# A two-layer encoder step in float32: expert token rows fetched by an indirect DMA, and expert weights split 2048 columns at a time into three pairs of buffers

## Chip, cores and metric

One NeuronCore of a Trainium2 chip runs the whole program. The metric is the device time of one execution in microseconds; lower is better. TensorE (PE) multiplies matrices, VectorE (DVE) and ScalarE (ACT) work element by element, GpSimd (POOL) and SyncE (SP) here mostly start DMAs.

## What is computed

The program is one inference step of a two-layer trunk on 256 prompt tokens and 32 sample tokens (288 columns, `TOK`), width 1024, all in float32. Each layer is a mixer with three gated branches and a feed-forward part; the second layer's feed-forward is a mixture of 8 experts, of which each token uses 2. The change concerns that last part:

```python
def moe(h, w_router, b_router, w1, w3, w2):
    logits = jnp.einsum('...d,de->...e', h, w_router) + b_router
    top_v, top_i = lax.top_k(logits, TOP_K)                 # TOP_K = 2 of N_EXPERTS = 8
    top_w = jax.nn.softmax(top_v, axis=-1)
    combine = jnp.einsum('...k,...ke->...e', top_w, jax.nn.one_hot(top_i, N_EXPERTS))
    y = None
    for e in range(N_EXPERTS):
        term = combine[..., e:e + 1] * swiglu(h, w1[e], w3[e], w2[e])   # w1, w3: 1024 x 3584, w2: 3584 x 1024
        y = term if y is None else y + term
    return y
```

## The kernel before, in words

**Float32 as two halves.** Every weight is used as a sum of a rounded part (`w_hi`) and a remainder (`w_lo`), both in the type float32r, and so is every activation. A product takes three matmuls: high by high, high by low, low by high. ACT makes `w_hi` (line 766 in the expert stage), DVE makes `w_lo` by a subtraction (line 1169), and PE multiplies.

**Jobs, turns, chunks.** The expert stage works through jobs. A job is one expert with up to 128 of its tokens (slots); with these inputs there are 8 jobs. A job has 7 turns (`TURNS`), a turn has two units of 256 hidden features, and a turn uses 6 weight matrices of 1 MB, each cut into two chunks of 1024 columns. PE takes the chunks of a turn in this order: `unit_rows(0)` chunks 0 to 3, `unit_down` chunks 4 and 5 (they belong to the unit before), `turn_hidden(0)`, `unit_rows(1)` chunks 6 to 9, `unit_down` chunks 10 and 11, `turn_hidden(1)`. A chunk is six matmuls of 512 columns.

**Buffers.** SP loads matrices into a ring of six 1 MB slots (`expert_ring`); a slot is loaded anew when DVE has split its second chunk. There are four `w_hi` and four `w_lo` buffers of 1024 columns (`CHUNKS`). ACT may round chunk c when PE has used chunk c-4. Within a turn ACT and DVE go through chunks 4 to 15, of which 12 to 15 are the first four of the next turn.

**Between the chunks**, in an order written out by hand in `turn_work`, ACT applies SiLU to the gate (`silu_unit`, line 944) when PE has finished `unit_rows`, DVE multiplies (`silu_times_g`, line 1518), PE transposes the result (`turn_hidden`, line 1929), ACT and DVE split it (`hidden_high`, `hidden_low`), and `unit_down` uses it. All engines run their own program in order and wait on semaphores.

**Job boundaries.** Results of job j are scaled and split in turn 0 of job j+1 (`sums_high`, `sums_low`) and scattered back to tokens by PE two row blocks at a time (`scatter`, line 1977), through the two `SPARE` PSUM banks. DVE adds each block to `x` (`add_rows`, line 1551) and so frees the bank. `scatter(2, 3)` at the head of turn 1 waits for `add_rows(0, 1)`, and `turn_spread` (line 1986) at its end waits for `add_rows(6, 7)`.

**Gathering tokens.** `spread` is a 0/1 matrix of tokens by slots. In turn 6 of a job, `gather(1)` (line 1887) multiplies it with the token rows `h_tok_hi` and `h_tok_lo`, 12 matmuls of 512 columns; ACT copies the result to `he_rows`, and `turn_rows` (line 1898) transposes it, since the experts want features on partitions. `gather(0)` does it for the first job right after the router. `low_rows` (line 1448) makes `h_tok_lo` on DVE within the router's chain.

Of the kernel before, what the change touches and what calls it, by code (L numbers as in the profile page):

```python
# [14 lines left out]
P = 128  # L15
D = 1024
DT = D // P
# [30 lines left out]
CHUNKS = 4  # L48
JOB_CHUNKS = 6 * UNITS
# [3 lines left out]
PEELED = 2  # L53
# [145 lines left out]
def number_groups():  # L199
# [8 lines left out]
    g.add([("logits",)] + [("htok", n, h) for h in range(2) for n in range(3)] + [("columns",), ("counts",)])  # L208
# [9 lines left out]
class Turns:  # L218
# [26 lines left out]
    def buffer(self, c):  # L245

        return (c - self.skipped(c)) % CHUNKS

# [8 lines left out]
def encoder(nc, x_t, vecs, w_in, cache_k_t, cache_v, ws_t, bs, g_v, bias_t, bias_s, w_branch, w_out,  # L257
            w1, w3, w2, router, router_b, e_w, y_t, k_t, v_t, z_state, vn_rows):
# [3 lines left out]
    with ctx:  # L262
# [3 lines left out]
        def sem(name):  # L266
# [17 lines left out]
        rows6 = sb("rows6", [P, 6, HALF])  # L284
# [28 lines left out]
        w_hi = [sb(f"w_hi{i}", [P, CHUNK_W], f32r) for i in range(CHUNKS)]  # L313
        w_lo = [sb(f"w_lo{i}", [P, CHUNK_W], f32r) for i in range(CHUNKS)]
# [15 lines left out]
        primed = sb("primed", [P, 1])  # L330
        rwg = sb("rwg", [P, DT, EXPERTS])
# [19 lines left out]
        h_tok_hi, h_tok_lo = sb("h_tok_hi", [P, 3, D], f32r), sb("h_tok_lo", [P, 3, D], f32r)  # L351
# [5 lines left out]
        rows_flat = rows6[:, :, :].rearrange("p a b -> p (a b)")  # L357
        sq = rows_flat[:, 0:DT * TOK].rearrange("p (a b) -> p a b", a=DT)
# [82 lines left out]
        htok_high, htok_low = sem("htok_high"), sem("htok_low")  # L441
        spread_ready, gathered, he_rows_ready, he_turned = (
            sem(n) for n in ("spread_ready", "gathered", "he_rows_ready", "he_turned"))
# [32 lines left out]
        def reader(name):  # L476
# [10 lines left out]
            if kind == "htok":  # L487
                return htok_low, 3 * at[1] + at[0] + 1
# [119 lines left out]
        def _(pool):  # L608
# [9 lines left out]
                           allow_small_or_imprecise_dtypes=True).then_inc(made, 1)  # L618
            pool.wait_ge(pool_step, 3)
# [45 lines left out]
            pool.wait_ge(state_stored, 64)  # L665


        @block.scalar
        def _(act):
# [99 lines left out]
            def drained_chunks(work, *chunks):  # L769
                at = turns.turn  # L770
                turns.turn, turns.drained = TURNS, True
                work(*chunks)
                turns.turn, turns.drained = at, False
# [1349 lines left out]
```

## Time and profile before

| | us |
|---|---|
| median of 3 runs | 1870.42 |
| lowest and highest of them | 1867.22 and 1872.52 |
| the profiled execution | 1872.94 |
| its span, first to last instruction | 1870.9 |
| what lies around the span | 2.0 |
| from the start of the first `gather` to the end of the span | 1047.1 |

The profile is of one execution. It lists each instruction with its start and its duration and, for an engine that stood idle, what ended the idle time. The expert stage takes more than half of the span and starts, with the first `gather`, at 823.81 us. PE is busy for 98% of the span and DVE for 77%; in the expert stage both are close to full. A matmul's busy time overlaps with that of the next one, so PE's stalls are better read from the starts of the weight loads (PEld) than from the busy share. "x6" behind an instruction means that six of its kind are merged in that row. The instructions of the spare and ring slots are the same operation on different buffers.

### The profile page before, as it was taken

What the parts mean: (1) busy time and instruction counts of PE and PEld (TensorE: products, weight loads), DVE (VectorE), ACT (ScalarE), POOL (GpSimd) and SP (SyncE); (2) the same over time, 40 slices, a digit from 0 to 9 for tenths busy, and PEclk for the clock granted to TensorE, in tenths of its full rate; (3) what the DMA queues carried; (4) which work ended last, traced back from release to release, by engine and by line L of the source; (5) the groups of instructions that cost most, each with busy time, mean ns of one, the idle gap of its engine ahead of it and who ended that gap; (6) DMA issues with size and microseconds to landing.
All of it is one profiled execution on the core that took longest, in us unless ns stands there. A gap on an engine that the chain in (4) does not pass through costs nothing.

```text
span 1870.9 us, 30255 instructions
## 1 busy us (share of the span) xinstructions
PE 1828.3 (98%) x10461; PEld 1601.4 (86%) x10461; DVE 1441.1 (77%) x1930; ACT 1165.0 (62%) x1551; POOL 24.7 (1%) x46
## 2 busy tenths in 40 slices
PE   8999999999999999989999999999999999999997
PEld 8999999999998999957878788788788787887886
DVE  7563557766665645549989989899899898998997
ACT  5444445333455433438877777778778777777785
POOL 3000000000000000000000000000000000000000
PEclk9999999999999999979999999999999999999999
DMA  8444533444544334148989989889899899898993
GB/s 333 150 136 143 196 136 140 168 172 153 180 148 150 113 136 158 68 180 339 374 320 345 373 317 353 330 336 365 335 340 376 319 345 373 313 355 322 345 375 134
DMA packets 68816, 479.05 MB, mean 256 GB/s; under 512 B 7888, under 2 KB 9936, under 8 KB 11520
## 3 DMA queue, kind: packets, MB, share of 16 engines
q1 hardware_dynamic: 66256, 469.00, 67.0%
q0 software_dynamic: 2336, 8.90, 1.4%
q8 instruction: 55, 0.90, 0.2%
q14 instruction: 25, 0.20, 0.0%
q10 hardware_dynamic: 144, 0.04, 0.0%
HBM read 474.23 MB, written 3.69 MB: 255 GB/s over the span
## 4 chain that ended last, share of the span: by engine, by line
PE 88%; DVE 7%; issue 3%; ACT 1%; DVEq 0%; DMA 0%; SPq 0%; ACTq 0%
PE psum L1939 14%; PE psum L1782 12%; PE psum L1784 12%; PE psum L1783 12%; PE psum L1919 10%; PE psum L1921 10%; PE psum L1920 10%; DVE w_lo L1169 2%; PE psum L1887 2%; PE psum L1929 1%; PE psum L1642 1%; DVE w_lo L1091 1%; PE psum L1977 0%; ACT w_hi L766 0%; PE psum L1898 0%
## 5 line engine op out<-in xcount | busy, mean ns | idle before, releaser
L1169 DVE TENSOR_TENSOR w_lo<-ring,w_hi 128x1024 fp32r<-128x1024 f32 x448 | 541.2, 1224 | 47.1 <-ACT w_hi L766 18.5
L766 ACT ACTIVATE w_hi<-ring 128x1024 fp32r<-128x1024 f32 x448 | 475.4, 1065 | 113.2 <-PE psum L1921 86.2
L1091 DVE TENSOR_TENSOR w_lo<-ring,w_hi 128x1024 fp32r<-128x1024 f32 x218 | 266.4, 1224 | 250.2 <-ACT w_hi L681 250.2
L681 ACT ACTIVATE w_hi<-ring 128x1024 fp32r<-128x1024 f32 x218 | 230.6, 1060 | 338.1 <-PE psum L1784 336.1
L1919 PE MATMUL psum<-w_hi,h_hi 128*128 128x512 f32 x896 | 359.8, 402 | 0.7 <-ACT h_hi L960 0.7
L1921 PE MATMUL psum<-w_hi,h_lo 128*128 128x512 f32 x896 | 351.0, 392 | 0.0
L1920 PE MATMUL psum<-w_lo,h_hi 128*128 128x512 f32 x896 | 350.1, 391 | 0.0
L1782 PE MATMUL psum<-h_hi,w_hi 128*128 128x288 f32 x1120 | 336.8, 301 | 11.6 <-DVE h_lo L1202 7.0
L1783 PE MATMUL psum<-h_lo,w_hi 128*128 128x288 f32 x1120 | 332.2, 297 | 0.0
L1784 PE MATMUL psum<-h_hi,w_lo 128*128 128x288 f32 x1120 | 331.2, 296 | 0.0
L1169 DVE TENSOR_TENSOR w_lo<-spare,w_hi 128x1024 fp32r<-128x1024 f32 x224 | 271.6, 1223 | 45.5 <-ACT w_hi L766 43.1
L766 ACT ACTIVATE w_hi<-spare 128x1024 fp32r<-128x1024 f32 x224 | 237.2, 1063 | 61.7 <-PE psum L1921 38.0
L1782 PEld LDWEIGHTS psum<-h_hi,w_hi 128*128 128x128 f32 x1120 | 211.7, 189 | 17.5 <-issue 9.7
L1784 PEld LDWEIGHTS psum<-h_hi,w_lo 128*128 128x128 f32 x1120 | 212.6, 190 | 0.0
L1783 PEld LDWEIGHTS psum<-h_lo,w_hi 128*128 128x128 f32 x1120 | 212.2, 190 | 0.0
L1921 PEld LDWEIGHTS psum<-w_hi,h_lo 128*128 128x128 f32 x896 | 168.7, 188 | 36.9
L1919 PEld LDWEIGHTS psum<-w_hi,h_hi 128*128 128x128 f32 x896 | 168.9, 189 | 33.2 <-ACT h_hi L960 1.0
L1920 PEld LDWEIGHTS psum<-w_lo,h_hi 128*128 128x128 f32 x896 | 169.4, 189 | 32.3
L1939 PE MATMUL psum<-w_hi,hid_hi 128*128 128x512 f32 x444 | 137.7, 391 | 0.0
L1939 PE MATMUL psum<-w_lo,hid_hi 128*128 128x512 f32 x444 | 137.2, 390 | 0.0
L1939 PE MATMUL psum<-w_hi,hid_lo 128*128 128x512 f32 x444 | 137.0, 390 | 0.0
L1939 PEld LDWEIGHTS psum<-w_hi,hid_lo 128*128 128x128 f32 x444 | 83.3, 188 | 17.9
(274 smaller groups left out, 2220.0 us busy)
## 6 DMA issues: line engine op xcount, KB each, us to landing
ring<-in_e_w SPq DMA_DIRECT2D x224, 1024.0 KB, 4.8
spare<-in_e_w SPq DMA_DIRECT2D x112, 1024.0 KB, 4.9
ring<-in_w_in SPq DMA_DIRECT2D x56, 1024.0 KB, 4.8
ring<-in_w SPq DMA_DIRECT2D x33, 1024.0 KB, 4.8
ring<-in_w_branch SPq DMA_DIRECT2D x12, 1024.0 KB, 4.8
ring<-in_w_out SPq DMA_DIRECT2D x8, 1024.0 KB, 4.8
bias<-in_bias_t POOLq DMA_DIRECT2D x2, 1024.0 KB, 9.9
x<-in_x_t SPq DMA_DIRECT2D x4, 288.0 KB, 3.9
```

Of the source, the lines that this page charges most:

```text
L681: nc.scalar.activation(dst, src, ACT.Copy).then_inc(rounded, 1)
L766: nc.scalar.activation(w_hi[turns.buffer(c)][:, :], expert_ring[s][:, c % 2 * CHUNK_W:(c % 2 + 1) * CHUNK_W], ACT.Copy).then_inc(rounded, 1)
L1091: nc.vector.tensor_tensor(low, src, high.bitcast(f32), ALU.subtract).then_inc(split, 1)
L1169: nc.vector.tensor_tensor(w_lo[buf][:, :], expert_ring[s][:, c % 2 * CHUNK_W:(c % 2 + 1) * CHUNK_W], w_hi[buf][:, :].bitcast(f32), ALU.sub ...
L1782: nc.tensor.matmul(bank(name), high, high_src[k], start=(k == 0), stop=False)
L1783: nc.tensor.matmul(bank(name), high, low_src[k], start=False, stop=False)
L1784: ins = nc.tensor.matmul(bank(name), low, high_src[k], start=False, stop=(k == tiles - 1))
L1887: ins = nc.tensor.matmul(psum[:, SPARE[hf], :], spread[0:rows, n, :], source[0:rows, n, cols], start=(n == 0 and source is h_tok_hi), stop ...
L1919: nc.tensor.matmul(out, he_hi[:, k, :], w_high, start=(k == 0), stop=False)
L1920: nc.tensor.matmul(out, he_hi[:, k, :], w_low, start=False, stop=False)
L1921: ins = nc.tensor.matmul(out, he_lo[:, k, :], w_high, start=False, stop=(k == DT - 1))
L1939: ins = nc.tensor.matmul(psum[:, SUMS[hf], :], h_part[:, b, :], w_part[:, hf * 512:(hf + 1) * 512], start=(first and b == 0 and w_part is ...
```

## The change

Token rows are written once to DRAM (`token_rows`, 288 rows and a row of zeros), by three DMAs on ACT's queue. For each job PE multiplies `spread` with a column of token numbers (`find_rows`, three matmuls with one column), DVE turns the result into integers (`row_numbers`), and POOL starts an indirect DMA that reads the rows named there from DRAM into `he_rows`. This replaces the 12 matmuls of `gather`, ACT's copies in `gathered_rows` and DVE's `low_rows`. For a later job `find_rows(1)` stands in turn 2 in place of turn 6, and the third turn is peeled off the loop for it. On DVE `row_numbers(1)` stands in turn 2 between the chunk pairs 4 and 6. In all 12 indirect DMAs are issued, as many as there can be jobs.

The expert weights are rounded and subtracted 2048 columns at a time (`round_pair`, `low_pair`), which is a whole matrix or two chunks, into three pairs of buffers: six chunks, where there were four. The third `w_lo` pair lies over `rows6`, and the third `w_hi` pair takes the room of `h_tok_lo`. The dense layers still split 1024 columns at a time in the first four buffers.

```diff
 CHUNK_W = 1024
 CHUNKS = 4
+EXPERT_CHUNKS = 6
...
-PEELED = 2
+PEELED = 3
...
     def buffer(self, c):
-        return (c - self.skipped(c)) % CHUNKS
+        return (c - self.skipped(c)) % EXPERT_CHUNKS
...
+            pool.wait_ge(rows_written, 48)
+            for job in range(MAX_JOBS):
+                pool.wait_ge(slot_row_ready, job + 1)
+                if job:
+                    pool.wait_ge(gathered, 16 * job)
+                nc.gpsimd.indirect_dma_start(he_rows, None, token_rows, bass.IndirectOffsetOnAxis(ap=slot_row[:, 0:1], axis=0),
+                                             bounds_check=TOK).then_inc(gathered, 16)
+            pool.wait_ge(gathered, 16 * MAX_JOBS)
...
+            def round_pair(c, drained=False):
+
+                at, s = turns.turn, c // 2 % EXPERT_RING
+                turns.turn, turns.drained = (TURNS, True) if drained else (at + c // TURN_CHUNKS, False)
+                c %= TURN_CHUNKS
+                act.wait_ge(slot_loaded[s], turns.loads(s, slot_before[s]))
+
+                act.wait_ge(chunk_used, turns.chunk(c + 1, EXPERT_CHUNKS))
+                nc.scalar.activation(hi_pairs[turns.buffer(c) // 2][:, :], expert_ring[s][:, 0:2 * CHUNK_W], ACT.Copy).then_inc(rounded, 2)
                 turns.turn, turns.drained = at, False
...
             act.wait_ge(token_scale, 1)
-            for hf in range(2):
-                for n, (t0, rows) in enumerate(TILES):
-                    evacuate(("htok", n, hf), h_tok_hi[0:rows, n, hf * 512:(hf + 1) * 512], rows, 512, htok_high,
+            for n, (t0, rows) in enumerate(TILES):
+                for hf in range(2):
+                    evacuate(("htok", n, hf), h_tok[0:rows, n, hf * 512:(hf + 1) * 512], rows, 512, htok_ready,
                              scale=rstd_tok[0:rows, n:n + 1])
+                act.wait_ge(htok_ready, 2 * n + 2)
+                if n == 2:
+                    act.wait_ge(zero_row, 1)
+                    rows += 1
+                act.dma_start(token_rows[t0:t0 + rows, :], h_tok[0:rows, n, :]).then_inc(rows_written, 16)
...
             def turn_work(t, last=False):
                 turns.turn = t
                 if not (turns.first and t == 0):
-                    round_chunks(4, 5)
-                round_chunks(6)
+                    round_pair(4)
+                round_pair(6)
                 silu_unit(0)
-                round_chunks(7)
-                if t == TURNS - 1 and not last:
-                    gathered_rows(1)
-                round_chunks(8, 9)
+                round_pair(8)
                 if t == 0 and not turns.first:
                     sums_high()
                 hidden_high(0)
-                round_chunks(10, 11)
+                round_pair(10)
                 if not last:
-                    round_chunks(12)
+                    round_pair(12)
...
                 if not last:
-                    round_chunks(13, 14, 15)
-                else:
-                    drained_chunks(round_chunks, 5)
+                    round_pair(14)
                 hidden_high(1)
...
+            def row_numbers(after):
+
+                dve.wait_ge(rows_found, turns.value(after + 1, 1))
+                nc.vector.tensor_scalar(slot_row[:, :], psum[:, SPARE[1], 0:1], float(TOK), None, ALU.add).then_inc(slot_row_ready, 1)
...
                 if t == 1 and boundary:
                     add_rows(2, 3)
                 if not (turns.first and t == 0):
-                    low_chunks(4, 5)
-                low_chunks(6)
+                    low_pair(4)
+                if t == 2:
+                    if following:
+                        row_numbers(1)
+                    else:
+                        nc.vector.memset(top[0:1, 0:1], 0.0).then_inc(slot_row_ready, MAX_JOBS)
+                low_pair(6)
                 silu_times_g(0)
-                low_chunks(7, 8, 9)
+                low_pair(8)
...
                 if not last:
-                    low_chunks(12)
+                    low_pair(12)
                 else:
-                    drained_chunks(low_chunks, 4)
+                    low_pair(4, True)
                 silu_times_g(1)
                 if t == TURNS - 1 and not last:
                     gathered_low(1)
                 if not last:
-                    low_chunks(13)
-                else:
-                    drained_chunks(low_chunks, 5)
+                    low_pair(14)
                 if boundary and t < 2:
                     add_rows(*((0, 1) if t == 0 else (6, 7)))
-                if not last:
-                    low_chunks(14, 15)
                 hidden_low(1)
...
                 unit_rows(0)
-                if t == TURNS - 1 and not last:
-                    gather(1)
+                if t == 2 and not last:
+                    find_rows(1)
```

**DVE at the end of turn 0 of a later job.** Before, DVE's rows from the product of unit 1 (line 1518) to the first chunk after the two additions read as follows. `w_lo3<-ring0` is chunk 13, `x<-x,psum` are `add_rows(0, 1)`, and `w_lo0<-ring1` is chunk 14.

```order
L1518 TENSOR_TENSOR h<-h,psum 128x256
L1167 REGISTER_ALU
L1169 TENSOR_TENSOR w_lo3<-ring0,w_hi3 128x1024
L1549 ISA
L1550 REGISTER_ALU
L1551 TENSOR_TENSOR x<-x,psum 128x288
L1549 REGISTER_ALU
L1550 REGISTER_ALU
L1551 TENSOR_TENSOR x<-x,psum 128x288
L1167 REGISTER_ALU
L1169 TENSOR_TENSOR w_lo0<-ring1,w_hi0 128x1024
```

In the changed kernel the same place reads so (line 1537 is the product, 1204 the subtraction, 1570 the addition, 1541 `hidden_low`):

```order
L1537 TENSOR_TENSOR h<-h,psum 128x256
L1202 REGISTER_ALU
L1204 TENSOR_TENSOR w_lo0<-ring1,w_hi0 128x2048
L1568 ISA
L1569 REGISTER_ALU
L1570 TENSOR_TENSOR x<-x,psum 128x288
L1568 REGISTER_ALU
L1569 REGISTER_ALU
L1570 TENSOR_TENSOR x<-x,psum 128x288
L1541 TENSOR_TENSOR hid_lo<-psum,hid_hi 128x256
```

One subtraction of 1024 columns stood between the product and the additions, and now one of 2048; chunks 14 and 15, which came behind the additions, now come ahead of them. At the end of turn 1 the same holds for `add_rows(6, 7)`.

**PE between `unit_rows(0)` and `unit_down`.** Before, in turn 6, the gather stands there (line 1921 is the last matmul of `unit_rows(0)`, 1939 is `unit_down`):

```order
L1921 MATMUL psum<-w_hi1,h_lo 128x512
L1872 ISA
L1887 MATMUL psum<-h_tok_hi,bm_lo 128x512 x3
L1887 MATMUL psum<-h_tok_lo,bm_lo 128x512 x3
L1887 MATMUL psum<-h_tok_hi,bm_lo 128x512 x3
L1887 MATMUL psum<-h_tok_lo,bm_lo 128x512 x3
L1934 REGISTER_ALU
L1903 REGISTER_ALU
L1939 MATMUL psum<-w_hi2,hid_hi 128x512 x2
```

In the changed kernel turn 6 has nothing there, and turn 2 has `find_rows` (line 1932 is the last matmul of `unit_rows(0)`, 1950 is `unit_down`):

```order
L1932 MATMUL psum<-w_hi0,h_lo 128x512
L1892 ISA
L1895 MATMUL psum<-token_id,bm_lo 128x1 x3
L1914 REGISTER_ALU
L1950 MATMUL psum<-w_hi1,hid_hi 128x512 x2
```

Twelve matmuls of 512 columns have become three of one column, four turns earlier.

## Rows read from the trace of the kernel before

**Rows 1.** The page: busy time, share of the span and instructions of each engine.

```profile
PE 1828.3 (98%) x10461; PEld 1601.4 (86%) x10461; DVE 1441.1 (77%) x1930; ACT 1165.0 (62%) x1551; POOL 24.7 (1%) x46
```

**Rows 2.** Chain that ended last, whole span: start, length, what.

```profile
823.81 7.54 PE psum L1887 x12
...
943.39 4.16 PE psum L1887 x12
...
1285.38 2.72 PE psum L1939 x12
1302.22 2.72 PE psum L1939 x12
...
1711.26 4.16 PE psum L1887 x12
```

**Rows 3.** Windows: length, busy time by engine, PE clock, DMA share, GB/s.

```profile
1199.55:1327.48 127.93, 127.47 (x578) 103.14 (x578) 116.64 (x131) 99.36 (x118) 0.00 (x0) 1.00 0.91 342
1216.00:1254.00 38.00, 37.54 (x177) 30.62 (x175) 37.13 (x46) 30.08 (x37) 0.00 (x0) 1.00 0.91 347
```

**Rows 4.** Timeline of PE's weight loads, turns 1 and 2 of a job.

```profile
1234.04 0.19 PEld L1977 LDWEIGHTS psum<-bm_hi,ac_hi 128*128 128x128 f32 x1 [0.67 <-DVE x L1551]
...
1234.53 0.19 PEld L1977 LDWEIGHTS psum<-bm_hi,ac_hi 128*128 128x128 f32 x1 [0.19 <-DVE x L1551]
...
1252.99 0.20 PEld L1986 LDWEIGHTS psum<-ident,bm_lo 128*128 128x128 f32 x2 [0.26 <-DVE x L1551]
...
1253.54 0.83 PEld L1988 LDWEIGHTS psum<-wsel,bm_lo 128*128 128x128 f32 x6
```

**Rows 5.** DVE's expert subtraction, all of them: min/median/max in ns.

```profile
L1169 DVE TENSOR_TENSOR w_lo<-ring,w_hi x448: 1214/1225/1228, 800.5 to 1848.8; 128x1024 fp32r<-128x1024 f32 x150
```

**Rows 6.** Timeline of DVE: a short operation, then turns 0 and 1 of that job.

```profile
817.92 0.18 DVE L1422 TENSOR_TENSOR gate<-gate 128x24 f32<-128x24 f32 x1
...
1228.67 2.35 DVE L1169 TENSOR_TENSOR w_lo<-spare,w_hi 128x1024 fp32r<-128x1024 f32 x2
...
1233.54 0.94 DVE L1551 TENSOR_TENSOR x<-x,psum 128x288 f32<-128x288 f32 x2
...
1250.38 0.41 DVE L1518 TENSOR_TENSOR h<-h,psum 128x256 f32<-128x256 f32 x1
1250.86 1.23 DVE L1169 TENSOR_TENSOR w_lo<-ring,w_hi 128x1024 fp32r<-128x1024 f32 x1
1252.00 0.94 DVE L1551 TENSOR_TENSOR x<-x,psum 128x288 f32<-128x288 f32 x2
```

**Rows 7.** Timeline of ACT, same turns.

```profile
1226.81 2.01 ACT L766 ACTIVATE w_hi<-spare 128x1024 fp32r<-128x1024 f32 x2
...
1230.13 0.39 ACT L944 ACTIVATE h<-psum 128x256 f32<-128x256 f32 x1 [0.29 <-PE psum L1921]
...
1249.49 0.38 ACT L944 ACTIVATE h<-psum 128x256 f32<-128x256 f32 x1 [0.29 <-PE psum L1921]
1249.77 1.05 ACT L766 ACTIVATE w_hi<-ring 128x1024 fp32r<-128x1024 f32 x1
```

**Rows 8.** Timelines at the first job: DVE, and PE's weight loads.

```profile
823.04 0.67 DVE L1463 TENSOR_SCALAR bm_lo<-slot_id,place 128x128 fp32r<-128x128 f32 x3
...
831.27 1.57 PEld L1898 LDWEIGHTS psum<-ident,bias 128*128 128x128 f32 x8 [0.44 <-issue]
833.89 0.28 PEld L1919 LDWEIGHTS psum<-w_hi,h_hi 128*128 128x128 f32 x1 [1.05 <-ACT h_hi L960]
```

**Rows 9.** Windows at the first job, columns as in rows 3.

```profile
824.00:828.00 4.00, 4.00 (x7) 1.82 (x8) 3.62 (x18) 0.00 (x0) 0.00 (x0) 0.50 0.00 0
```

**Rows 10.** DMAs from POOL's queue: number, KB each, median us to landing.

```profile
out_v_t<-gate POOLq DMA_DIRECT2D x2, 576.0 KB, 5.0
...
spare<-in_cache_v POOLq DMA_DIRECT2D x2, 512.0 KB, 14.2
```

**Rows 11.** Timeline of POOL, one DMA issue.

```profile
594.16 0.77 POOL L653 DMA_DIRECT2D out_v_t<-gate  x1 [47.06 <-ACT gate L733]
```

More of the change, by code:

```diff
@@ L207, in number_groups @@
     g.add(mixer_groups(1))
-    g.add([("logits",)] + [("htok", n, h) for h in range(2) for n in range(3)] + [("columns",), ("counts",)])
+    g.add([("logits",)] + [("htok", n, h) for n in range(3) for h in range(2)] + [("columns",), ("counts",)])
     g.next = 6
@@ L357, in encoder @@
         rows_flat = rows6[:, :, :].rearrange("p a b -> p (a b)")
+        lo_pairs.append(spare_lo)
+        w_hi, w_lo = ([pair[:, i * CHUNK_W:(i + 1) * CHUNK_W] for pair in pairs for i in range(2)] for pairs in (hi_pairs, lo_pairs))
         sq = rows_flat[:, 0:DT * TOK].rearrange("p (a b) -> p a b", a=DT)
@@ L949, in hidden_high @@
                                      ACT.Copy).then_inc(e_hi_ready, 1)
-            def gathered_rows(after):
-                for hf in range(2):
-                    act.wait_ge(gathered, turns.value(2 * after + hf + 1, 2))
-                    nc.scalar.activation(he_rows[:, hf * 512:(hf + 1) * 512], psum[:, SPARE[hf], :], ACT.Copy
-                                         ).then_inc(he_rows_ready, 1)
             def gathered_high(after):
@@ L1176, in low_chunks, with low_pair @@
                     turns.turn = at
-            def drained_chunks(work, *chunks):
-                at = turns.turn
-                turns.turn, turns.drained = TURNS, True
-                work(*chunks)
+            def low_pair(c, drained=False):
+                at, s = turns.turn, c // 2 % EXPERT_RING
+                turns.turn, turns.drained = (TURNS, True) if drained else (at + c // TURN_CHUNKS, False)
+                c %= TURN_CHUNKS
+                dve.wait_ge(rounded, turns.chunk(c + 1))
+                pair = turns.buffer(c) // 2
+                nc.vector.tensor_tensor(lo_pairs[pair][:, :], expert_ring[s][:, 0:2 * CHUNK_W], hi_pairs[pair][:, :].bitcast(f32),
+                                        ALU.subtract).then_inc(split, 2)
                 turns.turn, turns.drained = at, False
@@ L1830, in _ @@
             give(ins)
-            for hf in range(2):
-                pe.wait_ge(plain_ready, 4 * hf + 4)
-                for n, (t0, rows) in enumerate(TILES):
+            pe.wait_ge(plain_ready, DT)
+            for n, (t0, rows) in enumerate(TILES):
+                for hf in range(2):
                     take(("htok", n, hf))
@@ L1868, in _, with find_rows, turn_rows @@
             pe.wait_ge(count_ready, 1)
-            def gather(after):
+            def find_rows(after):
                 pe.wait_ge(spread_ready, turns.value(3 * (after + 1), 3))
+                plain = spread.bitcast(f32)
+                for n, (t0, rows) in enumerate(TILES):
+                    ins = nc.tensor.matmul(psum[:, SPARE[1], 0:1], plain[0:rows, n, :], token_id[0:rows, n:n + 1],
+                                           start=(n == 0), stop=(n == 2))
+                ins.then_inc(rows_found, 1)
+            def turn_rows(after):
                 if after:
@@ L2022, in job_work @@
                 turn_work(TURNS - 1, last)
-            gather(0)
+            pe.wait_ge(htok_ready, 6)
+            find_rows(0)
             turn_rows(0)
```

71 lines of the change are left out of this document (27 added, 44 removed).

## The prediction, made before the changed kernel was run

> **What bounds the kernel now.** I read the page's busy table first [rows 1]: PE is busy 98% of the span, DVE 77%, ACT 62%, and POOL nearly nothing. A cut on PE should then show in the time, and a cut on DVE or ACT only where PE waits for them. Then the chain that ended last [rows 2], for where the gathers are and how long a plain turn takes. The later seven gathers stand at 943.39 to 1711.26 us, one a job, at 4.16 us each; the first, at the start, takes 7.54 us. Two equal places in neighbouring turns lie at 1285.38 and 1302.22, so a plain turn takes 16.84 us. The windows [rows 3] then show a whole job: 127.93 us, with DVE busy for 116.64. In the 38 us of turns 0 and 1 DVE is busy for 37.13. That is the stretch to look at closely: DVE has no room there, and PE depends on it. The timeline of PE's weight loads [rows 4] shows the price today: PE waits for DVE's additions at the head of turn 1 (0.67 us, of which a part is the ordinary gap between two loads, then 0.19) and at its end (0.26).
>
> **Durations of the new pieces.** A subtraction of 1024 columns takes 1.225 us [rows 5] and one of 24 columns 0.18 [rows 6]; that is 1.04 ns a column, so 2048 columns take 1.225 + 1.07 = 2.29 us. After a single one the next operation begins 1.14 us later (1250.86 to 1252.00) [rows 6], 0.08 before its end, and two in a row last 2.35. So a pair occupies DVE for 2.21, against 2 x 1.14 = 2.28: a gain of 0.07, practically nothing. ACT does two chunks in a row in 2.01 [rows 7]; I take 1.92 for a pair, one fixed cost less. The Trainium skill, "VectorE: DVE Perf Modes", section on the TRN2 errata, gives (N+151)/0.96 ns for a float32 tensor_tensor. By it a pair would take 2.291 us; the trace agrees at 1024 columns (1.224 by the formula) and shows no 2048. So widening hardly makes anything cheaper. What it changes is the grain: a consumer waits for 2048 columns instead of 1024.
>
> **Plain turns.** Let PE start a turn at 0. Two chunks, 12 matmuls, take 2.72 us [rows 2], so one takes 1.36 and the two `turn_hidden` share the rest, 0.26 each. A tight pair is chunks 4 and 5: ACT starts after `hidden_high(1)`, at some 0.6, DVE at 2.6, done at 4.9; PE wants chunk 4 at 5.44. The product for `turn_hidden(0)` waits behind pair 6 on DVE and is ready at 7.7; PE wants it at 8.16. All margins come out at 0.45 us or more, so plain turns keep 16.84. DVE's work is hidden by that much and no more.
>
> **Gather out, find in.** Seven later gathers go: 7 x 4.16 = -29.1 us. ACT's copies go too, in ACT's idle time. Seven `find_rows` come, one a job for jobs 1 to 7. The nearest row is line 1988, also three float32 matmuls with one column on the same stationary tiles, 0.83 us [rows 4]. I take 0.84, so +5.9. Bounds: nothing if it slips into a stall, 1.3 if switching number types costs more.
>
> **A new wait in turn 2.** DVE stands at `row_numbers(1)` until PE has done `find_rows`, 0.84 + 0.25 us after `unit_rows(0)`; behind it wait pair 6 (2.21) and the product (0.41) [rows 6]. With 0.16 for itself they end 3.9 to 4.0 us after `unit_rows(0)`. PE reaches `turn_hidden(0)` after 0.84 + 2.72 = 3.56. A stall of 0.4, seven times: +2.7. Bounds 0 and 1.
>
> **The end of turn 1.** Here the grain shows. Before [rows 6, 7]: SiLU starts at 1249.49, one round at 1249.77, one subtraction at 1250.86, the two additions at 1252.00, and PE goes on at 1252.99 [rows 4], having waited 0.26. After: a pair in place of each single chunk. ACT's step until DVE may start was 1.09 and becomes 1.96; DVE's step until the additions was 1.14 and becomes 2.21. Together 1.94 us later, and PE has nothing else to do. Seven boundaries: +13.6. The lower bound is 0, if the extra two chunks of lead were to hide it; but round 14 may start only when chunk 9 is used, by the new distance of six as much as chunk 13 by the old one of four, so the lead gives nothing here.
>
> **The head of turn 1.** The same exchange ahead of `add_rows(0, 1)`. In the trace DVE is behind there: the additions start at 1233.54, although SiLU starts at 1230.13 [rows 6, 7]. By ACT's chain alone they would now start at 1230.13 + 0.28 + 1.96 + 2.21 = 1234.6, 1.0 later. By DVE's own queue, 12 chunks stand ahead of them where 10 did: 6 x 2.21 - 10 x 1.14 = +1.9. I take 1.6, between them and nearer to the second since DVE is busy all through: +11.2. Another 0.2 a boundary goes where pair 4 of turn 0 is late behind `gathered_low`: +1.2.
>
> **The first job.** The spread matrix is ready at 823.71 in both [rows 8]. PE is at half clock (0.50) [rows 9], so `find_rows` takes up to twice its 0.84, some 1.4 us; DVE has the numbers at 825.5 and POOL starts. The trace shows no indirect DMA. The nearest is POOL's store of 576 KB, 5.0 us from issue to landing; the other end is 14.2 us, for a load queued behind six others [rows 10]. I take 6, since nothing is ahead of it. Then `turn_rows` starts at 831.6 instead of 831.27 [rows 8]: +0.3. Bounds -1 and +8. The row stores on ACT's queue are issued by 822 and hidden by `find_rows` if they land in 3.5 us. In turn 0 of this job chunk 8 comes as a pair behind SiLU: +0.4.
>
> **Sum.** -29.1 + 5.9 + 2.7 + 13.6 + 11.2 + 1.2 + 0.7 = +6.2 us on the profiled execution's 1872.9, so 1879.1. That execution lies 2.5 above the median of the three runs, so against the median I forecast 1876.6, rounded to 1877. A measurement of this kernel can tell about 0.3% (5.6 us) from no change.
>
> **The rivals.** (1) *The gathers' time comes out.* If DVE and ACT kept up at both ends of turn 1, the sum would be -19.8, about 1851. For it: PE is 98% busy and 29 us of its work go. Against it: the order of DVE's rows, and DVE's 37.13 of 38 [rows 3]. If one of the two terms is absent, the sum is -5 to -7.5: 1863 to 1866.
>
> (2) *POOL and DVE get in each other's way.* The indirect DMA's issue falls into the densest part of DVE's work. If one subtraction a job is held up for as long as an issue takes, 0.77 [rows 11], and PE's margin of 0.45 is already used in turn 2, that is +5: 1882. It decides from 0.45 us a job on. The Trainium skill, "SBUF — State Buffer", in the box on DVE blocking SWDGE and the lines above it, says that DVE and GpSimd lock a shared port pair against each other, and that a DVE operation with two SBUF inputs, as `low_pair` is, contends with a GpSimd operation that reads SBUF. Against it: the subtraction never took more than 1.228 us [rows 5], though no POOL DMA was issued in the expert stage.
>
> (3) *The first indirect DMA is slow.* At 12 us it costs +6: 1883. PE then stands idle and goes on at half clock.
>
> (4) *Loads come late.* DMA's share is 0.91 [rows 3], the indirect reads add 0.5 MB to 42 MB a job (7 turns of 6 MB), and in the last job four spare DMAs come at once. If ACT waited 2 us a job for a slot, 1891. Against it: a slot is free 16.84 - 1.96 - 2.21 = 12.7 us before it is wanted.
>
> **How the numbers follow.** Forecast as worked, 1870 to 1883: 0.46. Rival 1 whole 0.06, half 0.20. Rival 2 0.10, rival 3 0.12, rival 4 0.06. Faster by over 0.3% (under 1864.8): rival 1 whole and half of its half form, 0.17. Slower by over 0.3% (above 1876): rivals 2 to 4 nearly whole, 0.26, and half of the forecast, 0.24, together 0.50. Within: the rest, 0.33. The range leaves out rival 1 whole and rival 4 and little else: 1861 to 1888. The forecast's own is 1870 to 1883.
>
> **What would show it.** A job of 128 to 129 us, where -3.3 on PE is given back; PE's weight load at the head of turn 1 waiting for an addition for some 2.1 us, and the one at its end for 2.2; plain turns at 16.84; DVE subtractions of 2.29; in turn 2 a stall near 0.4. Wrong would be: a job near 124.5, waits under 1 us at the additions (rival 1); subtractions above 2.35 while POOL issues (rival 2); `turn_rows(0)` after 834 (rival 3); ACT waiting for a ring DMA (rival 4).

## The result, and the profile after

| | before | after |
|---|---|---|
| median, us | 1870.49 (4 runs) | 1901.67 (4 runs) |
| lowest and highest | 1867.22, 1872.52 | 1897.20, 1902.56 |
| span of the profiled execution | 1870.9 | 1899.1 |

The ratio is 1.0164, with a 95% interval of 1.0142 to 1.0186: 31 us slower. The forecast was 1877 and its range ended at 1888. The direction was right; 25 us are missing from the sum. One of the four executions of e6 below ran in a slow state (3258.87 us, granted clock 0.72) and is left out of e6's figures.

The page of the kernel after, busy time by engine, answers to [rows 1]:

```profile
PE 1823.5 (96%) x10413; PEld 1602.8 (84%) x10413; DVE 1401.6 (74%) x1600; ACT 1096.3 (58%) x1201; POOL 50.6 (3%) x59
```

PE has less work and yet ends later, so it stands idle or runs slowly. The chain and the waits of the kernel after say where it stands idle. This is the view of waits over the expert stage (us in total, times, longest), first of the kernel after:

```profile
PEld psum L1997 <- DVE x L1570: 15.8, 7, 2.3
PEld psum L1988 <- DVE x L1570: 15.5, 14, 2.0
```

and then of the kernel before, the same two places, there lines 1986 and 1977:

```profile
PEld psum L1977 <- DVE x L1551: 5.8, 14, 0.7
...
PEld psum L1986 <- DVE x L1551: 1.9, 7, 0.3
```

`turn_spread` at the end of turn 1 waits 13.9 us more, `scatter(2, 3)` at its head 9.7 more. That is 23.6 of the forecast 24.8. The order on DVE that makes it so is in its timeline, at the end of turn 1 of job 2:

```profile
1125.89 2.29 DVE L1204 TENSOR_TENSOR w_lo<-ring,w_hi 128x2048 fp32r<-128x2048 f32 x1 [0.36 <-ACT w_hi L797]
1128.10 0.42 DVE L1537 TENSOR_TENSOR h<-h,psum 128x256 f32<-128x256 f32 x1
1128.85 2.29 DVE L1204 TENSOR_TENSOR w_lo<-ring,w_hi 128x2048 fp32r<-128x2048 f32 x1 [0.34 <-ACT w_hi L797]
1131.06 0.94 DVE L1570 TENSOR_TENSOR x<-x,psum 128x288 f32<-128x288 f32 x2
```

The product ends at 1128.5, ACT's rounding of pair 14 ends at 1128.8, the subtraction follows, and only then come the two additions. Now the timeline of PE's weight loads, both ends of that turn 1, against [rows 4]:

```profile
1110.96 0.19 PEld L1988 LDWEIGHTS psum<-bm_hi,ac_hi 128*128 128x128 f32 x1 [2.02 <-DVE x L1570]
...
1111.69 0.19 PEld L1930 LDWEIGHTS psum<-w_hi,h_hi 128*128 128x128 f32 x1
1111.82 0.19 PEld L1931 LDWEIGHTS psum<-w_lo,h_hi 128*128 128x128 f32 x1
1112.05 0.19 PEld L1932 LDWEIGHTS psum<-w_hi,h_lo 128*128 128x128 f32 x1
...
1132.05 0.20 PEld L1997 LDWEIGHTS psum<-ident,bm_lo 128*128 128x128 f32 x2 [2.26 <-DVE x L1570]
...
1133.44 0.29 PEld L1930 LDWEIGHTS psum<-w_hi,h_hi 128*128 128x128 f32 x1
1133.61 0.34 PEld L1931 LDWEIGHTS psum<-w_lo,h_hi 128*128 128x128 f32 x1
1134.04 0.33 PEld L1932 LDWEIGHTS psum<-w_hi,h_lo 128*128 128x128 f32 x1
...
1136.60 0.30 PEld L1932 LDWEIGHTS psum<-w_hi,h_lo 128*128 128x128 f32 x1
1136.94 0.19 PEld L1930 LDWEIGHTS psum<-w_hi,h_hi 128*128 128x128 f32 x1
1137.17 0.19 PEld L1931 LDWEIGHTS psum<-w_lo,h_hi 128*128 128x128 f32 x1
```

The reader is to look at the distances behind each wait. After the one at 1110.96 the loads of `unit_rows(0)` follow each other by 0.23 us. After the one at 1132.05 they are 0.43 apart (1133.61 to 1134.04), until 1136.94. The windows of the kernel after, columns as in [rows 3], name the reason:

```profile
1129.00:1133.40 4.40, 2.38 (x15) 1.75 (x13) 3.30 (x4) 2.19 (x2) 0.00 (x0) 1.00 0.98 361
1133.40:1136.80 3.40, 3.40 (x10) 2.74 (x10) 3.25 (x6) 0.00 (x0) 0.00 (x0) 0.50 0.59 246
1136.80:1140.00 3.20, 3.20 (x15) 2.60 (x15) 0.22 (x1) 1.87 (x1) 0.00 (x0) 1.00 0.50 151
```

The granted clock is 0.50 for 3.4 us: TensorE is at 1.2 GHz instead of 2.4, right after a stretch in which it was busy for 2.38 of 4.40 us. It then does 10 matmuls where the next 3.2 us hold 15. The trace of after has 11 such stretches in the later jobs, one at the start of every turn 2 and, in jobs 1, 3, 5 and 7, one at the start of turn 1. The trace of before has none between the first job and the end of the last. The sum of the forecast has no term for this.

Turn lengths follow from the first weight load of `unit_rows(0)` in successive turns (in the rows above 1111.69 to 1133.44, so 21.75):

| length in us | before | after |
|---|---|---|
| turn 0 of a later job | 18.85 | 20.34 |
| turn 1 | 19.61 | 21.75, or 23.31 with half clock |
| turn 2 | 16.84 | 19.54 |
| turns 3, 4, 5 | 16.84 each | 17.02, 16.99, 16.97 |
| turn 6 | 22.11 | 18.00 |

So plain turns (3, 4 and 5) are longer too, by 0.13 to 0.18 us. That was not forecast either.

### The profile page after: what moved, and what is told of

Its sections match the earlier page's. It is cut to its first block, busy times and chain, and to the rows that moved or that the text cites. A ratio compares the mean times of both kernels' runs of the same rounds, so it can differ in the third digit from the quotient of the medians.

```text
span 1899.1 us, 29260 instructions
## 1 busy us (share of the span) xinstructions
PE 1823.5 (96%) x10413; PEld 1602.8 (84%) x10413; DVE 1401.6 (74%) x1600; ACT 1096.3 (58%) x1201; POOL 50.6 (3%) x59
## 3 DMA queue, kind: packets, MB, share of 16 engines
q10 hardware_dynamic: 476, 1.22, 0.2%
## 4 chain that ended last, share of the span: by engine, by line
PE 87%; DVE 5%; issue 4%; ACT 2%; DMA 1%; DVEq 0%; ACTq 0%; SPq 0%; POOLq 0%
PE psum L1950 13%; PE psum L1802 12%; PE psum L1804 12%; PE psum L1803 12%; PE psum L1930 11%; PE psum L1931 10%; PE psum L1932 10%; ACT w_hi L797 2%; DVE w_lo L1204 1%; PE psum L1940 1%; PE psum L1662 1%; DVE w_lo L1109 1%; DVE ac_lo L1557 1%; DVE x L1570 1%; PE psum L1909 0%
## 5 line engine op out<-in xcount | busy, mean ns | idle before, releaser
L1204 DVE TENSOR_TENSOR w_lo<-ring,w_hi 128x2048 fp32r<-128x2048 f32 x222 | 508.0, 2291 | 82.6 <-ACT w_hi L797 81.1
L797 ACT ACTIVATE w_hi<-ring 128x2048 fp32r<-128x2048 f32 x222 | 426.2, 1920 | 139.1 <-PE psum L1932 134.3
L1109 DVE TENSOR_TENSOR w_lo<-ring,w_hi 128x1024 fp32r<-128x1024 f32 x218 | 266.7, 1225 | 250.0 <-ACT w_hi L701 249.7
L701 ACT ACTIVATE w_hi<-ring 128x1024 fp32r<-128x1024 f32 x218 | 230.6, 1060 | 336.3 <-PE psum L1804 333.3
L1930 PE MATMUL psum<-w_hi,h_hi 128*128 128x512 f32 x896 | 369.5, 412 | 2.2 <-DVE h_lo L1548 1.0
L1931 PE MATMUL psum<-w_lo,h_hi 128*128 128x512 f32 x896 | 359.5, 401 | 0.0
L1932 PE MATMUL psum<-w_hi,h_lo 128*128 128x512 f32 x896 | 359.1, 401 | 0.0
L1204 DVE TENSOR_TENSOR w_lo<-spare,w_hi 128x2048 fp32r<-128x2048 f32 x112 | 256.6, 2291 | 31.0 <-ACT w_hi L797 31.0
L797 ACT ACTIVATE w_hi<-spare 128x2048 fp32r<-128x2048 f32 x112 | 214.1, 1911 | 0.1
L1930 PEld LDWEIGHTS psum<-w_hi,h_hi 128*128 128x128 f32 x896 | 173.4, 194 | 40.8 <-DVE w_lo L1204 2.0
```

What stands on the lines that cost most here:

```text
L701: nc.scalar.activation(dst, src, ACT.Copy).then_inc(rounded, 1)
L797: nc.scalar.activation(hi_pairs[turns.buffer(c) // 2][:, :], expert_ring[s][:, 0:2 * CHUNK_W], ACT.Copy).then_inc(rounded, 2)
L1109: nc.vector.tensor_tensor(low, src, high.bitcast(f32), ALU.subtract).then_inc(split, 1)
L1204: nc.vector.tensor_tensor(lo_pairs[pair][:, :], expert_ring[s][:, 0:2 * CHUNK_W], hi_pairs[pair][:, :].bitcast(f32), ALU.subtract).then_in ...
L1930: nc.tensor.matmul(out, he_hi[:, k, :], w_high, start=(k == 0), stop=False)
L1931: nc.tensor.matmul(out, he_hi[:, k, :], w_low, start=False, stop=False)
```

## The experiments

On the three chips used for the experiments the kernel before had medians of 1870.0 to 1872.3 us, so the ratio to it is given for each experiment.

### e1: the additions ahead of the pair

```diff
-                if not last:
-                    low_pair(14)
                 if boundary and t < 2:
                     add_rows(*((0, 1) if t == 0 else (6, 7)))
+                if not last:
+                    low_pair(14)
```

> The changed kernel with one move on VectorE: at a boundary the additions (0,1) and (6,7) stand ahead of the subtraction of pair 14 instead of behind it. The two new waits of TensorE, 2.2 to 2.3 us each at both ends of turn 1, should shrink by the 2.2 us of a pair, to a few tenths. Theory (a wait of about 2 us is followed by 3.4 us at half clock): the half-clock stretches go with the waits, so the time falls by 31 us of waits and by some 15 to 18 us of half clock, to 1853 to 1858 us. Rival (the half clock has another cause, such as the DMA's or GpSimd's work): only the waits go, 1870 us, and stretches of granted clock 0.50 still stand in turns 1 and 2.

Measured: 1852.79 us (1850.68 to 1854.36), ratio to before 0.9905 [0.9888, 0.9921]. A move of two small additions is worth 48.9 us (1901.67 to 1852.79). In DVE's timeline the order is now product, additions, subtraction:

```profile
1242.16 0.41 DVE L1537 TENSOR_TENSOR h<-h,psum 128x256 f32<-128x256 f32 x1
1242.49 0.93 DVE L1570 TENSOR_TENSOR x<-x,psum 128x288 f32<-128x288 f32 x2
1243.35 2.28 DVE L1204 TENSOR_TENSOR w_lo<-ring,w_hi 128x2048 fp32r<-128x2048 f32 x1
```

and `turn_spread` no longer waits. The windows of one whole job (1.00 is the granted clock), to be read with PE's 124.60 busy of 124.60:

```profile
1207.60:1332.20 124.60, 124.60 (x573) 101.94 (x571) 111.80 (x90) 90.80 (x75) 2.41 (x1) 1.00 0.93 358
```

No half-clock stretch is left in the later jobs. The additions were late because of the pair in front of them, and 48.9 is 17.6 more than the 31.3 us of waits that went. Those 17.6 could still be something else that this order removes; e2 separates them.

### e2: the same waits, but TensorE kept busy

```diff
+            def fill(count):
+                for _ in range(count):
+                    nc.tensor.matmul(psum[:, GATED[0], 0:TOK], he_hi[:, 0, :], spread_t, start=True, stop=True)
...
                 if t == 1 and boundary:
+                    fill(15)
                     scatter(2, 3)
...
                 if t == 1:
+                    if boundary:
+                        fill(16)
                     turn_spread()
```

> The changed kernel, with extra matmuls on TensorE that use nothing new and whose results nobody reads: 15 of 288 columns ahead of the additions' wait at the head of turn 1 and 16 ahead of the one at its end. They fill the two waits of 2.2 us without removing them (VectorE gets there no earlier). Theory (idle TensorE makes the clock fall): no stretch of granted clock 0.50 stands in turns 1 and 2, and the time falls by 15 to 18 us, to 1884 to 1887. Rival (the clock falls for something else that happens in these turns): stretches and time stay, 1900 to 1904, or slightly more, since the filler's own end may be later than VectorE's.

Measured: 1884.70 us (1882.32 to 1887.23), 17.0 less than after, by doing more. PE's weight loads at the same end of turn 1 in e2:

```profile
1129.97 2.14 PEld L2006 LDWEIGHTS psum<-bm_hi,h_hi 128*128 128x128 f32 x16
1132.26 0.20 PEld L1997 LDWEIGHTS psum<-ident,bm_lo 128*128 128x128 f32 x2
...
1133.64 0.19 PEld L1930 LDWEIGHTS psum<-w_hi,h_hi 128*128 128x128 f32 x1
1133.75 0.19 PEld L1931 LDWEIGHTS psum<-w_lo,h_hi 128*128 128x128 f32 x1
1133.99 0.19 PEld L1932 LDWEIGHTS psum<-w_hi,h_lo 128*128 128x128 f32 x1
...
1151.63 0.19 PEld L1930 LDWEIGHTS psum<-w_hi,h_hi 128*128 128x128 f32 x1
```

`turn_spread` starts no earlier than in after, turn 1 lasts 21.75 us as there (1111.89 to 1133.64), but the loads behind it follow at 0.24, and turn 2 lasts 17.99 (1133.64 to 1151.63) instead of 19.54. No stretch at 0.50 is left in turns 1 and 2. A stretch costs 1.55 (19.54 - 17.99), or 1.56 in turn 1 (23.31 - 21.75); eleven make 17.1, and 17.0 came back. So it is the idle TensorE that loses the clock, and neither the indirect DMA nor the pairs.

### e6 and e9: the same wait in the kernel before

e6 puts the additions behind chunks 14 and 15 in the kernel before, e9 behind chunk 14 alone.

```diff
-                if boundary and t < 2:
-                    add_rows(*((0, 1) if t == 0 else (6, 7)))
                 if not last:
                     low_chunks(14, 15)
+                if boundary and t < 2:
+                    add_rows(*((0, 1) if t == 0 else (6, 7)))
```

> The kernel before, gathers on TensorE and chunks of 1024, with one move on VectorE: at a boundary the additions (0,1) and (6,7) stand behind the subtractions of chunks 14 and 15. TensorE then waits for them at both ends of turn 1 for two subtractions, 2.3 us, longer, 14 times, which is 32 us less what is given back by the two subtractions being done already: 1885 to 1900 by the waits alone. Theory (such waits make the clock fall): stretches of granted clock 0.50 appear in turns 1 and 2 of the later jobs, as in the changed kernel, and add 15 to 20 us: 1900 to 1920. Rival (the clock falls only beside the indirect DMA or the pairs): no such stretches, at most 1900.

> The kernel before with the additions (0,1) and (6,7) behind chunk 14 alone, one subtraction later than before and one earlier than in e6. The waits of TensorE at both ends of turn 1, 0.67 and 0.26 us in the kernel before and 3.0 and 3.3 in e6, should come out near 1.8 and 1.6. By the waits alone 14 x 1.14 = 16 us more, and up to 5 for what ScalarE does later: 1886 to 1892. If waits of this length are also followed by half clock, another 10 to 20 us: 1897 to 1912. It tells from which length of a wait the clock falls.

Measured: e6 1928.70 us (three executions, 1928.35 to 1929.48), ratio 1.0309 [1.0288, 1.0330]; e9 1893.77 us, ratio 1.0117 [1.0101, 1.0132]. The kernel of before, whose gathers and chunks nobody touched, loses 58 us by late additions. e6 came out above both expectations: its two waits a boundary add up to 44.6 us, 36.9 more than before, where I had 32 less something given back; the other 21 to 22 fit the half clock, for which its trace shows ten stretches in the later jobs, four of them twice as long as those of after. The end of turn 1 in e6, PE's loads:

```profile
1002.98 0.20 PEld L1986 LDWEIGHTS psum<-ident,bm_lo 128*128 128x128 f32 x2 [3.28 <-DVE x L1551]
```

and in e9, with a window of the stretch that follows it by 2.8 us:

```profile
1129.89 0.20 PEld L1988 LDWEIGHTS psum<-ident,bm_lo 128*128 128x128 f32 x2 [1.90 <-DVE x L1551]
```

```profile
1133.00:1135.00 2.00, 2.00 (x6) 1.59 (x5) 0.73 (x1) 1.06 (x1) 0.00 (x0) 0.50 0.94 393
```

Here is what followed the waits at a boundary in six traces, seven boundaries each:

| kernel | wait at the head of turn 1, us | turn 1 at half clock | wait at its end, us | turn 2 at half clock |
|---|---|---|---|---|
| before | 0.67 | 0 of 7 | 0.26 | 0 of 7 |
| e9 | 1.5 to 1.85 | 0 of 7 | 1.90 | 3 of 7 |
| after | 2.02 | 4 of 7 | 2.26 | 7 of 7 |
| e6 | 2.8 to 3.0 | 3 of 7 | 3.28 | 7 of 7 |
| e2 | filled | 0 of 7 | filled | 0 of 7 |
| e1 | none | 0 of 7 | none | 0 of 7 |

From 1.90 us on a wait of TensorE at these two places can cost itself and some 1.6 us more; up to 1.85 it never did. Its length alone does not decide. Equal waits are not all followed by the half clock (the 2.02 at 1110.96 was not), and e6's waits of 2.8 to 3.0 us at the head of turn 1 are followed by it no more often than after's of 2.02. The seven waits of one place differ in nothing that these views show, so what picks them out stays open. e9 was expected at 1897 to 1912 if its waits were followed by half clock and at 1886 to 1892 if not; it lies between, with three of fourteen.

### e3: the indirect DMA alone

The chunks are 1024 columns again, in four buffers and in the order of before; only the token rows come by DMA.

```diff
-EXPERT_CHUNKS = 6
+EXPERT_CHUNKS = 4
...
-                    round_pair(4)
-                round_pair(6)
+                    round_chunks(4, 5)
+                round_chunks(6)
...
-                    low_pair(14)
+                    low_chunks(13)
...
+                if not last:
+                    low_chunks(14, 15)
```

> The indirect DMA alone: token rows by DMA as in the changed kernel, chunks of 1024 columns in four pairs of buffers and in the order of before. Theory (the wide pairs in front of the additions make both new waits and with them the half clock): the gathers' 29 us come out, less 5.9 for the seven finds and a small stall in turn 2: 1846 to 1850 us, jobs of about 124.6 us, no half-clock stretch in the later jobs, and plain turns tell whether the 0.14 us they lost come from the DMA (17.0) or from the pairs (16.84). Rival (the indirect DMA or its wait in turn 2 is what slows the job): above 1860.

Measured: 1850.87 us (1850.32 to 1852.06), ratio 0.9894 [0.9878, 0.9911]. One job in the windows of e3, and POOL's issue in it:

```profile
1208.70:1333.20 124.50, 124.04 (x575) 102.15 (x573) 116.65 (x132) 98.23 (x117) 1.27 (x1) 1.00 0.93 357
```

```profile
1254.55 1.27 POOL L683 DMA_INDIRECT bias<-token_rows,slot_row  x1 [123.17 <-DVE slot_row L1484]
```

The job takes 124.4 us against 127.93 [rows 3]; turn 6 is 4.40 shorter (22.11 to 17.71) and turn 2 0.89 longer (16.84 to 17.73). By itself this half of the change is a gain of 19.4 us (1850.87 against 1870.27). Plain turns are 16.84.

### e7, e11, e13, e14: where 0.14 us of a plain turn go

e7 is e3 over the six buffers, one chunk at a time. e11 is e3 with four of the six, the first pair and the third; the edit shown is what it adds to e3. e13 has only `w_hi` in the third pair's place, e14 only `w_lo`.

```diff
-        return (c - self.skipped(c)) % EXPERT_CHUNKS
+        b = (c - self.skipped(c)) % EXPERT_CHUNKS
+        led = self.first and self.turn == 0 and c < 4
+        return b if led or b < 2 else b + 2
```

and then for e13 `w_lo[4:6] = w_lo[2:4]`, for e14 `w_hi[4:6] = w_hi[2:4]`.

> The indirect DMA alone as in e3 (chunks of 1024 columns, one operation each, in the order of before), but over the six buffers of the changed kernel instead of four. It parts the two halves of the other change: the number and place of the buffers, and the width of an operation. e3 has plain turns of 16.84 us, the changed kernel 16.98. Width theory: plain turns stay 16.84 and the time stays that of e3, 1849 to 1852 us. Place theory: TensorE reads more slowly while VectorE and ScalarE write the six buffers where these lie, so plain turns are 16.98 and the time is 1854 to 1858.

> e3 (indirect DMA alone, single chunks, four buffers), but the four buffers are the first pair and the third, the one that the changed kernel adds in the memory of the mixer's rows, in place of the first and second. e3 has plain turns of 16.84 us and 1850.9, e7 with all six buffers 16.98 and 1855.6. If the place of the third pair slows TensorE's reads, plain turns are 16.9 to 17.0 here too and the time is 1853 to 1857 us. If it is the number of buffers, the distance between what is written and what is read, plain turns are 16.84 and the time is 1850 to 1852.

> e11 (single chunks over the first and the third pair of buffers, plain turns of 17.10 us) with only the upper halves w_hi in the third pair's place and the lower halves w_lo back in the second pair's. If the place of w_hi is what slows the reads, plain turns stay 17.0 to 17.1 and the time 1857 to 1860 us; if it is the place of w_lo, they are 16.84 and 1850 to 1852; if each has its share, 16.97 and 1854 to 1857.

> The complement of e13: only the lower halves w_lo in the third pair's place (the memory of the mixer's rows), w_hi in the second pair's. If w_lo's place is the cause, plain turns are 17.0 to 17.1 and the time 1857 to 1860 us; if w_hi's, 16.84 and 1850 to 1852; if each has its share, 16.97 and 1854 to 1857.

| kernel | buffers | plain turn, us | median, us | ratio to before |
|---|---|---|---|---|
| e3 | pairs 1, 2 | 16.84 | 1850.87 | 0.9894 [0.9878, 0.9911] |
| e7 | pairs 1, 2, 3 | 16.98 | 1855.60 | 0.9912 [0.9897, 0.9927] |
| e11 | pairs 1, 3 | 17.10 | 1860.29 | 0.9949 [0.9933, 0.9964] |
| e13 | `w_hi` 1, 3; `w_lo` 1, 2 | 17.10 | 1861.79 | 0.9939 [0.9923, 0.9956] |
| e14 | `w_hi` 1, 2; `w_lo` 1, 3 | 17.02 | 1855.87 | 0.9911 [0.9894, 0.9927] |

Two plain turns, the first load of `unit_rows(0)` in each, are shown by the loads of e3, e7 and e11 in that order:

```profile
1264.93 0.19 PEld L1948 LDWEIGHTS psum<-w_hi,h_hi 128*128 128x128 f32 x1
...
1281.77 0.19 PEld L1948 LDWEIGHTS psum<-w_hi,h_hi 128*128 128x128 f32 x1
```

```profile
1266.47 0.19 PEld L1948 LDWEIGHTS psum<-w_hi,h_hi 128*128 128x128 f32 x1
...
1283.45 0.19 PEld L1948 LDWEIGHTS psum<-w_hi,h_hi 128*128 128x128 f32 x1
```

```profile
1266.86 0.19 PEld L1950 LDWEIGHTS psum<-w_hi,h_hi 128*128 128x128 f32 x1
...
1283.96 0.19 PEld L1950 LDWEIGHTS psum<-w_hi,h_hi 128*128 128x128 f32 x1
```

Neither the width of an operation nor the number of buffers does it, but the memory of the third pair: e11 has as many buffers as e3, and its plain turns are, with e13's, the longest. The third outcome that had been named, a share for each half that adds up (16.97 alone), was not seen: `w_hi` there costs as much alone as both do (17.10), and `w_lo` alone 0.18. By the median of the plain turns, the 24 loads of `unit_rows` span 5.13 to 5.14 us in e3 and 5.18 to 5.22 in e7, e11, e13 and e14, twice a turn; that is all of e7's 0.14. In e11 `unit_down` with the transposes takes another 3.09 to 3.14 for 3.06; there, other than in e7, its chunks 4 and 5 lie in the third pair. Why that memory is slower for PE, and why `w_hi` or `w_lo` alone is enough in `unit_rows`, stays open; the second pair together with the third, without the first, was not tried. The Trainium skill, "SBUF — State Buffer", in the section on its ports, says that PE's ports never wait for anyone. The traces show no wait either, but the matmuls follow each other more slowly: an effect of the place of 0.8 to 1.5% of a plain turn, which that sentence alone would not let one expect. Whether a port takes part in it no run here shows.

### e8: two pairs instead of three

```diff
-EXPERT_CHUNKS = 6
+EXPERT_CHUNKS = 4
```

> The changed kernel with two pairs of buffers instead of three: 2048 columns at a time in the memory of four chunks. ScalarE may round a pair only when both of its chunks four places back are used, so every pair comes later than in the changed kernel. By the distances between the uses (1.36 us a chunk) the lead shrinks by 2.7 us where the margin was 0.45: waits of about 1 to 2 us in each half of every turn, 56 turns, 1960 to 2080 us, and many stretches at half clock where such waits are near 2 us. Rival (the third pair of buffers does nothing): 1902 us, plain turns 16.98.

Measured: 2277.26 us, ratio 1.2169 [1.2148, 1.2189], 20% above after. Plain turns are 23.1 to 25.0 us. PE's waits in e8 over the expert stage:

```profile
PEld psum L1950 <- DVE w_lo L1204: 140.5, 103, 2.4
PEld psum L1940 <- DVE h L1537: 114.4, 101, 2.2
PEld psum L1930 <- DVE w_lo L1204: 83.0, 63, 1.8
```

The waits are as long as expected, but there are about five in a turn where I had counted two. So the six buffers do something: in the memory of four chunks a grain of two cannot be fed, and the third pair is what lets the change run at all.

### e10 and e12: the additions one chunk earlier

e10 is e3 with the additions ahead of chunk 13, e12 the same move in the kernel before.

```diff
+                if boundary and t < 2:
+                    add_rows(*((0, 1) if t == 0 else (6, 7)))
                 if not last:
                     low_chunks(13)
                 else:
                     drained_chunks(low_chunks, 5)
-                if boundary and t < 2:
-                    add_rows(*((0, 1) if t == 0 else (6, 7)))
```

> e3 (the indirect DMA alone) with the additions (0,1) and (6,7) one subtraction earlier, ahead of chunk 13. In e3 TensorE still waits 0.7 us at the head of turn 1 and 0.3 at its end. If the additions are what it waits for, both waits nearly go: 7 jobs at 0.7 to 1.0 us less, 1844 to 1847 us. Rival (chunk 13 comes late in their place, since four buffers give no lead): 1850 us or more, with a wait for the subtraction in unit_rows.

> The kernel before with one move alone: the additions (0,1) and (6,7) one subtraction earlier, ahead of chunk 13. It parts what e10 gained: e10 is 1841.3 us, e3 with the additions in their old place 1850.9. If the move is worth the same without the indirect DMA, 1870.4 less 9.6, so 1860 to 1862 us, with TensorE's two waits at turn 1 nearly gone. If the gather in the last turn takes the gain, 1868 to 1871.

Measured: e10 1841.29 us (1838.40 to 1843.60), ratio 0.9834 [0.9821, 0.9848]; e12 1862.68 us, ratio 0.9960 [0.9947, 0.9974]. The job of e10 in the windows, PE busy without a gap:

```profile
1206.50:1329.80 123.30, 123.30 (x574) 102.05 (x573) 116.13 (x132) 98.27 (x117) 1.27 (x1) 1.00 0.93 360
```

Both waits at turn 1 are gone from the list of waits. Turn 0 is 17.91 instead of 18.85 and turn 1 19.36 instead of 19.61, 1.2 us a job, 8.3 in seven. From PE's first load of `find_rows` or `gather` to the end, e10's trace is 8.1 us shorter than e3's (1015.2 and 1023.3), and e12's 8.1 shorter than that of before (1039.1 and 1047.1); the medians differ by 9.6 and 7.3. So the move is worth the same with and without the indirect DMA. e10 is the fastest version: 29 to 31 us under before and 60 under after.

## Why the prediction was wrong

The runs split the 31 us into four parts. The third column has differences of medians (each good to some 3 us), the fourth those of the expert stage in the traces, from PE's first load of `gather` or `find_rows` to the end (1047.1 us before, 1075.5 after):

| part | runs | medians, us | stage, us |
|---|---|---|---|
| indirect DMA for gathers | e3 - before | -19.4 | -23.8 |
| place of the third pair | e7 - e3 | +4.7 | +6.7 |
| pairs in front of the additions, first job | e2 - e7 | +29.1 | +29.2 |
| half clock | after - e2 | +17.0 | +16.3 |

**Gather out, find in, turn 2, first job.** Forecast -29.1 + 5.9 + 2.7 + 0.3 = -20.2 (the other 0.4 of the 0.7 belongs to chunk 8), measured -19.4 by the medians. That they agree is partly luck. Turn 6 gained 4.40 rather than 4.16, and turn 2 lost 0.89, all of it `find_rows`: e3's trace has no wait there. In the later jobs that makes 7 x (0.89 - 4.40) = -24.6 for the forecast -20.5, and the trace of the stage says -23.8. The 4 us between the stage and the medians lie ahead of the stage or in the spread of executions: e3's stage began at 826.3 us and that of before at 823.8, but in e6 and e12, which are the kernel of before up to there, it began at 821.5 and 826.8. With pairs and a full clock (e1) turn 2 is 18.00 beside plain turns of 16.98, so some 0.1 beside the 0.89, where I had 0.4. In after DVE stands 4.4 us at `row_numbers` for 2.9 in e2; that difference is the half clock again.

**First indirect DMA.** `unit_rows(0)` of the first job starts at 834.42 instead of 833.89 [rows 8]: +0.5, forecast +0.3. Counted from the first load behind the spread matrix, it is 10.85 us instead of 10.11, +0.7, and in e1, e2, e3 and e7 +0.9 to +1.4. The two guesses behind the forecast were both off and nearly cancelled, which was luck. The chain of after (start, length):

```profile
821.49 4.76 DMA token_rows<-h_tok
...
827.29 4.47 DMA bias<-token_rows,slot_row
```

The row store took 4.76 us, so it was not hidden and POOL began 1.8 later than I had put it; the indirect DMA took 4.47 with its start instead of 6. Rival 3, a slow first DMA, did not happen.

**End and head of turn 1.** Forecast 13.6 and 11.2, measured 13.9 and 9.7. The choice of 1.6 at the head, between 1.0 and 1.9, came out at 1.4. The other 5.5 of the 29.1 lie in small pieces in turns 0, 1, 2 and 6 and in the first job, where I had 1.6 for pair 4 and chunk 8.

**The step that failed** is the one that costs a wait at its own length: "Together 1.94 us later, and PE has nothing else to do. Seven boundaries: +13.6." Fourteen waits of about 2 us were priced as idle time alone. Eleven of them were followed by a stretch at 1.2 GHz, 1.55 us each, 17.0 together. I had read the half clock at the first job [rows 9] and wrote under rival 3 that PE "stands idle and goes on at half clock", but used it for one long wait only and not for the fourteen that the sum itself had just made. With it the forecast would have been 1877 + 17 = 1894. The other 8 us are the third pair's place (4.7, the step below), 2.7 in the pairs' part (29.1 for 26.4) and 0.8 in that of the DMA.

**The second step that failed** is "so plain turns keep 16.84". The margins on DVE and ACT held, and no wait appeared in plain turns; the turns are longer since PE's matmuls follow each other more slowly with the third pair's memory. No row of before could show that.

**Rival 1** did not happen in this kernel; e1 shows what it would have taken: with the additions moved the waits went, and the time was 1852.8 where the rival said 1851. (Its share in "faster by over 0.3%" is 0.06 + 0.10 = 0.16, not 0.17.) **Rival 2** was wrong as put. The subtractions of the kernel after, all of them (min/median/max in ns):

```profile
L1204 DVE TENSOR_TENSOR w_lo<-ring,w_hi x221: 2271/2293/2297, 849.8 to 1874.9; 128x2048 fp32r<-128x2048 f32 x111
```

None is longer than 2.30 us, which is the 2.29 of the forecast. But POOL is held up by DVE, as its timeline in after shows beside e3's 1.27:

```profile
1142.40 2.40 POOL L683 DMA_INDIRECT bias<-token_rows,slot_row  x1 [128.25 <-DVE slot_row L1470]
...
1795.31 1.00 POOL L683 DMA_INDIRECT bias<-token_rows,slot_row  x1 [124.97 <-DVE top L1588]
```

The issue at 1142.40 began during the subtraction of 1141.63 to 1143.92, took 2.40 us and ended 0.88 behind it. In e3 it took 1.27 and ended 0.88 behind the single subtraction beside it (1253.72 to 1254.94), and at 1795.31, with DVE idle, it took 1.00. All ten issues that began beside a subtraction in after, and the ten in e3, ended 0.88 to 0.92 behind it. The Trainium skill, "SBUF — State Buffer", in its section on the ports, says that of the two the one that starts first keeps the shared pair for its whole instruction and the other waits. The rows agree where DVE was first. The other way round they show no wait: the next subtraction began at 1144.17, before the issue ended at 1144.80, and took 2.29 as well:

```profile
1141.63 2.29 DVE L1204 TENSOR_TENSOR w_lo<-ring,w_hi 128x2048 fp32r<-128x2048 f32 x1
...
1144.17 2.29 DVE L1204 TENSOR_TENSOR w_lo<-spare,w_hi 128x2048 fp32r<-128x2048 f32 x1
```

It costs nothing here, since the rows are wanted four turns later. **Rival 4** did not happen: no wait of ACT for a ring DMA is among its waits in after. Loads land in 5.7 to 6.1 us there and 6.8 to 7.0 in e3, which is faster all the same.

## What to carry to other kernels

A wait of TensorE near 2 us can cost more than its length: look at the granted clock and at the distances of the weight loads right behind it, and add the slow stretch to the sum, with its own uncertainty, since not every such wait brings one. When the grain of a producer is doubled, list what is queued behind it and move the small operations that another engine waits for ahead of it; here two additions decided between 1902 and 1853 us. Test two changes that come in one diff apart: the indirect DMA alone gained 19 us, and the wider pairs hid it; even with the additions moved (e1, 1852.8) they brought nothing that singles in four buffers (e3, 1850.9) did not have.

## What was not expected of the hardware

- TensorE's granted clock fell to 0.50 for 3.4 us at a time (in e6 also 6.8) at waits of 1.90 to 3.28 us; at the job boundaries it never did at those up to 1.85, and not at each of equal length.
- Matmuls of the same shape and order are slower by 0.8 to 1.5% of a turn when `w_hi` or `w_lo` lies in other SBUF memory, without any wait in the trace.
- An indirect DMA of 128 rows of 4 KB landed 4.5 us after its start while nothing else was loading. Its issue on POOL took 1.0 us with VectorE idle, and 1.27 and 2.40 beside subtractions of 1.22 and 2.29 us, ending 0.88 us behind the subtraction in both.
